# Attention loop of a two-layer hybrid encoder: one unit per step against two units per step

## The reference, cut to what matters

```python
h = layer_norm(x, ln_in_g, ln_in_b)                       # 512 tokens x 1024
for l in range(2):
    a_q, a_k, a_v, b_u, b_b, b_c, c_u, d_q, d_k, d_v = split_columns(h @ w_in[l])
    out_a = windowed_gqa_sink(a_q, a_k, a_v, sink[l])     # 4 heads, window 128, bias by distance, sink
    out_b = short_conv_mixer(b_u, b_b, b_c, conv_w[l])
    out_c = fourier_mixer(c_u)
    out_d = dense_gqa_blocks(qd, kd, d_v)                 # 4 heads, all 512 keys
    mix = concat(rms_norm(o, g_i) for o in (out_a, out_b, out_c, out_d))
    h = layer_norm(ALPHA * h + mix @ w_out[l], ...)
    h = layer_norm(ALPHA * h + square(relu(h @ w1[l])) @ w2[l], ...)
```

## Time and profile before

| | us |
|---|---|
| median of three runs | 1141.22 (1141.08 to 1141.42) |
| the profiled execution's own time | 1143.06 |
| its span, first to last instruction | 1141.4 |
| PE busy in the span | 1117.7 (98%) |
| DVE, ACT, POOL busy | 607.1 (53%), 392.0 (34%), 89.1 (8%) |
| attention loop, layer 0: first scores to first MLP matmul | 100.54 |
| attention loop, layer 1 | 101.65 |
| PE idle in the span by the page's waits (L406, L556, L362, L574, L371) | 16.3 |

### The profile page before, as it was taken

How to read it: one execution, slowest core, us unless ns; L and a number is a source line. 1 busy time by engine, 2 the same in 40 slices (tenths; PEclk the granted TensorE clock), 3 DMA queues, 4 the chain that set the end, 5 groups by cost and what they waited for, 6 DMA issues and landing times.

```text
span 1141.4 us, 15090 instructions
## 1 busy us (share of the span) xinstructions
PE 1117.7 (98%) x5486; PEld 932.9 (82%) x5486; DVE 607.1 (53%) x906; ACT 392.0 (34%) x630; POOL 89.1 (8%) x80
## 2 busy tenths in 40 slices
PE   6999999999999999999999999999999999999997
PEld 5787788898888888888888878879888888888886
DVE  6754876855235235235657467677533433434446
ACT  2433655452143133134134246543421421422320
POOL 4200222000000000000002002221000000000001
PEclk9999999999999999999999999999999999999999
DMA  7322112033114113124104420211323123222201
GB/s 288 145 105 83 38 56 75 1 118 148 74 74 148 74 74 147 74 74 148 74 3 148 148 74 20 74 38 45 148 74 146 76 74 130 85 78 110 85 28 74
DMA packets 16944, 104.90 MB, mean 92 GB/s; under 512 B 2096, under 2 KB 2528, under 8 KB 5232
## 3 DMA queue, kind: packets, MB, share of 16 engines
q1 hardware_dynamic: 15408, 97.92, 23.2%
q0 software_dynamic: 1184, 5.86, 1.6%
q10 hardware_dynamic: 288, 0.27, 0.1%
HBM read 100.90 MB, written 2.10 MB: 90 GB/s over the span
## 4 chain that ended last, share of the span: by engine, by line
PE 90%; DVE 4%; issue 2%; ACT 1%; DVEq 0%; ACTq 0%
PE bank L362 27%; PE bank L364 27%; PE bank L363 27%; PE bank L574 2%; PE bank L556 2%; PE bank L471 1%; PE bank L547 1%; PE bank L371 1%; PE bank L548 1%; ACT stage L827 1%; DVE mx L1194 1%; DVE stage L1191 1%; DVE x L949 0%; DVE x L1154 0%; DVE mx L1200 0%
## 5 line engine op out<-in xcount | busy, mean ns | idle before, releaser
L362 PE MATMUL bank<-h_hi,w_hi 128*128 128x512 f32 (+1 forms) x704 | 261.0, 371 | 1.6 <-DVE h_lo L970 1.6
L364 PE MATMUL bank<-h_hi,w_lo 128*128 128x512 f32 (+1 forms) x704 | 260.3, 370 | 0.0
L363 PE MATMUL bank<-h_lo,w_hi 128*128 128x512 f32 (+1 forms) x704 | 260.3, 370 | 0.0
L362 PE MATMUL bank<-w_hi,hid_hi 128*128 128x512 f32 x512 | 199.3, 389 | 0.0
L364 PE MATMUL bank<-w_hi,hid_lo 128*128 128x512 f32 x512 | 199.2, 389 | 0.0
L363 PE MATMUL bank<-w_lo,hid_hi 128*128 128x512 f32 x512 | 199.2, 389 | 0.0
L693 ACT CAST w_hi<-w_raw 128x2048 fp32r<-128x2048 f32 x60 | 112.3, 1908 | 243.9 <-PE bank L364 220.3
L362 PEld LDWEIGHTS bank<-h_hi,w_hi 128*128 128x128 f32 x704 | 132.6, 188 | 24.3 <-issue 1.8
L363 PEld LDWEIGHTS bank<-h_lo,w_hi 128*128 128x128 f32 x704 | 132.6, 188 | 22.5
L364 PEld LDWEIGHTS bank<-h_hi,w_lo 128*128 128x128 f32 x704 | 132.6, 188 | 22.4
L1259 DVE TENSOR_TENSOR x<-bank,x 128x512 f32<-128x512 f32 x64 | 44.2, 690 | 198.1 <-PE bank L364 197.7
(11 more groups left out here) (145 smaller groups left out, 1359.1 us busy)
## 6 DMA issues: line engine op xcount, KB each, us to landing
w_raw<-in_weights SPq DMA_DIRECT2D x86, 1024.0 KB, 4.8
rows<-in_rows POOLq DMA_DIRECT2D x4, 1024.0 KB, 5.0
w_raw<-in_weights SPq DMA_DIRECT2D x4, 512.0 KB, 6.9
out_h<-x SPq DMA_DIRECT2D x8, 256.0 KB, 2.0
x<-in_x SPq DMA_DIRECT2D x3, 512.0 KB, 7.4
dft<-in_dft SPq DMA_DIRECT2D x1, 1024.0 KB, 9.4
qk_gain<-in_qk_gain POOLq DMA_DIRECT2D x3, 192.0 KB, 3.4
dq_even<-dq_lo POOLq DMA_DIRECT2D x2, 256.0 KB, 2.9
```

What stands on the lines that cost most here:

```text
L362: pe.matmul(dst, s_hi, m_hi, start=first, stop=False)
L363: pe.matmul(dst, s_hi, m_lo, start=False, stop=False)
L364: return pe.matmul(dst, s_lo, m_hi, start=False, stop=last)
```

## The change

Steps now handle pairs of units. In step p PE makes the scores of units 2p and 2p+1, then the side items, then the values of the pair p-2, then (in even steps from 4) the turned quad, then the transposes of the pair p-1. ACT and DVE follow in kind. There are 16 pairs and 18 steps. `stage` has four places; the fourth lies over the first half of `bz`, which is free by then. The side table is written anew: two `w` items in each of the steps 0 to 11, in 13, 15 and 17, none in 12 and 14, the first turned block in step 16, the second in step 17. `mix_low` of the Fourier group is done for both halves in step 1, the query copies `dq_even` and `dq_odd` in step 3, the norm of the blocks 0 and 1 in the steps 14 to 16. On POOL the subtraction for `dq_lo` moves ahead of the first power of the quads.

```diff
-STAGES = 3
-TURN_LAG, VALUE_LAG = 1, 1
-STEPS = UNITS + VALUE_LAG
+STAGES = 4
+PAIRS = UNITS // 2
+STEPS = PAIRS + 2
...
 def quad_scaled_in(step):
-    q, rest = divmod(step - VALUE_LAG - 3, 4)
-    return q if rest == 0 and q >= 0 else None
+    return (step - 3) // 2 if step >= 3 and step % 2 else None
...
-SIDE_STEPS = {-1: [("s", 0)], 0: w_items(0, 0, 1), 4: [("s", 1)],
-              27: [("t", 0, 0), ("t", 0, 1)], 32: [("t", 1, 0), ("t", 1, 1)]}
...
+SIDE_STEPS = {-1: [("s", 0)]}
+for _g in range(3):
+    SIDE_STEPS.update({4 * _g + _t: w_items(_g, _t, _t + 1) for _t in range(TOK)})
+SIDE_STEPS[2] = SIDE_STEPS[2] + [("s", 1)]
+SIDE_STEPS.update({13: w_items(3, 0, 1), 15: w_items(3, 1, 2), 16: t_items(0), 17: w_items(3, 2, 3) + t_items(1)})
...
+                for p in range(STEPS):
+                    for u in pair(p):
+                        scores(u)
+                    for k in sides_of(p):
                         side(k)
-                    if quad_turned_in(s) is not None:
-                        turn_quad(quad_turned_in(s))
...
+                    for u in pair(p - 2):
+                        take_values(u)
+                    if quad_turned_in(p) is not None:
+                        turn_quad(quad_turned_in(p))
+                    for u in pair(p - 1):
+                        turn_probs(u)
...
+                for p in range(STEPS):
+                    if quad_turned_in(p) is not None:
+                        square_head_out(quad_turned_in(p))
+                    for u in pair(p):
+                        exponents(u)
+                    if p in (0, 1):
+                        wait(act, l, "fourier_out", p + 1)
                         wait(act, l, "square_sum", 1)
-                        square(j, co[:, j, :])
-                        mix_high(1, j, co[:, j, :])
...
+                        square(p, co[:, p, :])
+                        mix_high(1, p, co[:, p, :])
+                    for k in sides_of(p):
+                        side(k)
+                    if quad_turned_in(p) is not None:
+                        mix_high_quad(quad_turned_in(p))
+                    for u in pair(p - 1):
+                        copy_turned(u)
+                    if p == 3:
                         wait(act, l, "mix_lo", 2)
...
+                for p in range(STEPS):
+                    for u in pair(p):
+                        row_maximum(u)
+                    for k in sides_of(p):
                         side(k)
-                    if s in (2, 3):
-                        mix_low(1, s - 2, co[:, s - 2, :])
...
+                    if p == 1:
+                        mix_low(1, 0, co[:, 0, :])
+                        mix_low(1, 1, co[:, 1, :])
+                    if quad_turned_in(p) is not None:
+                        mix_low_quad(quad_turned_in(p))
+                    if quad_scaled_in(p) is not None:
+                        scale_quad(quad_scaled_in(p))
+                    if p == 14:
+                        centre(2 * l + 1, 0)
+                    if p == 15:
+                        scale(2 * l + 1, 0)
+                    if p == 16:
+                        centre(2 * l + 1, 1)
+                        scale(2 * l + 1, 1)
                 centre(2 * l + 1, 2)
```

More of the change, by code:

```diff
@@ L142 @@
 TAIL = len(SIDE)
-SIDE += w_items(3, 3, 4) + [("t", t, half) for t in (2, 3) for half in range(2)]
-NORM_AT = {24: 0, 28: 1}
+SIDE += w_items(3, 3, 4) + t_items(2) + t_items(3)
 def sides_of(step):
@@ new lines, in scores @@
+                def scores(u):
+                    in_d, j, kv, qb, k0, k1 = unit(u)
+                    if u == 0:
+                        wait(pe, l, "k_lo", 2)
+                    if u == 16:
+                        wait(pe, l, "k_lo", 4)
+                        wait(pe, l, "dq_moved", 32)
+                    if u >= 2:
+                        wait(pe, l, "probs", u - 1)
+                    q, k = slice(qb * P, (qb + 1) * P), slice(k0 * P, k1 * P)
+                    both = (dq_even, dq_odd)[kv][:, j, q] if in_d else aq[:, kv, j, q]
+                    dst = bank[u % 2][:, 0:(k1 - k0) * P]
+                    pe.matmul(dst, both, (dk_hi if in_d else ak_hi)[:, kv, k], start=True, stop=False)
+                    pe.matmul(dst, both, (dk_lo if in_d else ak_lo)[:, kv, k], start=False, stop=True).then_inc(sems["scores"], 1)
@@ L801, in split_half @@
                         done.then_inc(sems["w_hi"], 1)
[L803 to L832, removed]
-                        wait(act, l, "square_sum", 1)
-                        square(j, co[:, j, :])
-                        mix_high(1, j, co[:, j, :])
-                    if s in (5, 6):
-                        j = s - 5
-                        wait(act, l, "mix_lo", 2)
-                        wait(act, l, "dq_copied", j + 1)
-                        act.copy(dq_even[:, j, :], dq[:, j, :]).then_inc(sems["dq_hi"], 1)
-                        act.copy(dq_odd[:, j, :], dq[:, j, :]).then_inc(sems["dq_hi"], 1)
-                    for k in sides_of(s):
-                        side(k)
-                    if quad_turned_in(s) is not None:
-                        mix_high_quad(quad_turned_in(s))
-                    if s in (10, 11):
-                        split_half(12, s - 10, 24)
-                    if s in (18, 19):
-                        split_half(13, s - 18, 32)
@@ L1349, in _ @@
                         layer_norm_rstd(2 * l + 1, q - 5, q - 4)
-                    if q == 1:
+                    if q == 0:
+                        for j in range(2):
+                            wait(pool, l, "dq_hi", 2 * j + 2)
+                            pool.tensor_tensor(dq_lo[:, j, :], dq[:, j, :], dq_even[:, j, :].bitcast(F32), ALU.subtract).then_inc(sems["dq_lo"], 1)
                         wait(pool, l, "dq_lo", 2)
```

165 lines of the change are left out of this document (82 added, 83 removed).

## The result

The changed kernel took 1146.3 us (1143.44 to 1147.14, six executions) beside 1141.32 of the kernel before: ratio 1.0034, interval 1.0024 to 1.0045 (the quotient of the two medians, 1.0044, lies at its upper end). In a second measurement it was 1145.2 beside 1142.14, 1.0023 (1.0013 to 1.0032). The forecast was 1136.9. The profiled execution of after took 1143.44, its span 1141.8. Two executions with a mean granted clock of 0.44 and 0.85 (2558.97 us of the kernel before, 1248.76 of the last variant) are left out of every ratio.

A forecast was written before the change was run, and what follows sets the result against it. PE, busy 98% of the span, was taken as the bound. The two loops were to lose 10.2 us and clock drops to add 5.9, so 1141.22 - 4.3 = 1136.9 us; range 1130.5 to 1141.5.

The forecast's parts named there:

- 43 of 60 go, 3.65 us per layer: PE, both loops: 43 of 60 changes from f32 to r matmuls vanish, at 0.085 us each.
- Two Fourier remainders (0.66 each): DVE at the loop's start: two remainders of 0.66 us each, ending at 10.2, the second waiting for ACT.
- The stall before `s`: PE at the loop's start: item `s` waits 2.05 us for DVE's add of that step's first `w`.
- the lock: Rival: DVE's second remainder waits for POOL at the start, 1.1 us per layer, 1139.1 in all; chance 0.08.
- Four spans of 1.47: PE's clock drops once in each new stretch, at start and end of both loops, 4 x 1.47 = 5.9 us.
- The waits for ACT inside the loop: PE in steps 3 to 15: no wait for ACT; all 8.7 us of old stalls taken as gone.
- The end of the loop: From the scores of pair 15: new stalls of 4.5 us in sum.
- idle before the turned block 0: PE in step 16: waits 2.1 us for the first half of DVE's `scale`.
- a wait before the MLP: PE behind step 17's values: waits 1.9 us for DVE's adds with statistics and `h_lo` halves.
- the bound in the A steps: Rival: DVE takes PE's place there, A pairs keep 5.5 us instead of 5.2, 1140.5 in all; chance 0.12.
- The fourth stage: A smaller edit, said only to take waits away; priced at nothing.

The follow-up runs named there:

- the split of the groups: Kernel with all three moves, but in steps 8 to 11 PE's values stand between the two `w` items; step 11 took 6.36 us against 6.27.
- the last variant: Kernel with `s` in step 3, the end reordered and the second Fourier remainder in step 2, but `s` behind step 3's `w` items: ratio 0.9939.

## Why the prediction was wrong, step by step

**The ledger.** Forecast per loop with its clock 98.9, measured 102.5: 3.6 too much. To the start of step 4 it takes 24.65 (forecast 20.24 + 1.47), 2.9 too much; from there to the scores of pair 15, 58.48 (56.25), 2.2; from there to the MLP 19.34 (19.4 + 1.47), 1.5 too little. The parts 20.24 and 56.25 are the forecast's terms sorted by step.

**The step that failed: "43 of 60 go, 3.65 us per layer. It is the surest term."** The changes go, and each is worth its 0.09; the split of the groups shows it. But a pair gained 0.10, not 0.31 (6.38 - 6.07). I read one edge of an r group, where it starts late, and took the f32 distances of one unit (0.35, 0.80) as the price of the work in any grouping. In groups of two they are 0.80 and 1.73, 0.23 more per pair. At the price of these D pairs the missing 0.21 is some 3.4 us per layer over 16 pairs, an estimate, since the A pairs have shorter groups. The ledger leaves about 3.0 for it: the 2.2 of the middle, and 0.8 of the start's 2.9 when 0.8 of stall and 1.5 of clock are taken off and 0.2 added for the shorter waits of the scores 2 and 3. Either way it takes back most of the 3.65. That the order alone does this is shown with the other engines taken away. It is the largest part of the miss, 6 of 7.3 us in the two loops.

**"Two Fourier remainders (0.66 each)".** The stall before `s` was forecast at 2.05 and is 2.85. Without the overlap with POOL it is 1.69 of idle, about 1.85 by starts: the forecast's sum was right but for the lock, which stood among the rivals with 0.08 and a price of 1.1 per layer; holding POOL back gave 1.0. The row on which I rejected it was misread. I held POOL's 1.75 for its own length; by itself the addition takes 1.30 (the row above; before, the subtraction for `dq_lo` of the same shape takes 1.30 too). So the row, with DVE ahead by 0.13, is a POOL instruction held for 0.45 by DVE's remainder, and the trace of the kernel before already showed the lock. It also had the other order, a little earlier, with POOL's addition from 114.86 to 116.51 and DVE's remainders of another group, the first of which came behind it:

```profile
L1102 DVE SCALAR_TENSOR_TENSOR mix_lo<-bo,cols,mix_hi x2: 741/1251/1761, 115.3 to 117.0; 128x512 fp32r<-128x512 f32 x2
```

741 and 1761 ns, once more 1.0 too long. The Trainium skill, SBUF — State Buffer, section "SBUF: two separate sides", says that whichever of the two starts first keeps the shared ports for its whole instruction. The traces agree, in both orders: held DVE instructions end 0.55 after POOL's end (117.06 after 116.51, 129.33 after 128.78), and POOL's addition begun behind a DVE remainder takes 1.75 to 1.81 for 1.30.

**The clock.** Four spans of 1.47 were forecast, one at each start and end of two loops. What came is worth four such spans, but two in each layer's start, 3.0 behind the larger stall, and none at the end. That the sum of 6.0 meets the 5.9 is luck. That the drop hangs on the idle and not on the small products alone is shown: filled, it is gone; at 1.00 of idle it costs 1.6 (131.62 to 136.44 is 4.82, at the full level 3.2), at 1.69 it costs 1.6 or 3.2, at 2.70 it costs 3.0. The idle alone doesn't fix it: 0.77 ahead of the scores of pair 3 was followed by a drop in layer 1 and by none in layer 0 of the same profile. At a loop's end it appeared in one profile only (the item `s` one step later, layer 0).

**What was right.** The waits for ACT inside the loop are gone. The end of the loop is right in sum (19.34), less so in its parts: 1.4 of idle before the turned block 0 for 2.1, and the turned block 1 waits for the adds of step 17 (0.37 and 0.73), which I had priced as a wait before the MLP. DVE did not become the bound in the A steps. The fourth stage is worth nothing.

**What stays open.** The 3.6 per loop make 7.3 of the 9.4 between forecast and result. The loops' growth of 2.9 accounts for the second measurement, but the first had 5.0 between the medians. What differs between profiles outside the loops lies ahead of the first one: between the loops every profile shows 456.9 to 457.2, behind the second 361.4 to 361.6, but the first loop begins anywhere from 118.21 to 121.93, in kernels whose work up to there is the same. It begins by 119.7 where the granted clock is 1.00 from 16 to 28 us, and from 119.9 on where it is low there. An estimate from this: had the median execution of after begun its loop as the profiled one of before did, it would have taken 1143.44 + 2.63 = 1146.1, and 1146.3 was measured; the six of the kernel before, 1141.0 to 1141.65, lie 1.4 to 2.1 below its profiled one, as with an earlier start. No profile of such an execution shows it, and why an execution gets the one or the other start was not found. The low clock of before in layer 1 isn't constant either: with the fourth stage alone both loops last 100.5, so between loops without a drop in before the change costs 4.0, not 2.9.

## What to carry to other kernels

Price a reordering by measuring the whole pattern both ways, not one edge of it: an f32 group of twice the length costs more than two short ones. When work of one queue moves, ask what the engine that shares its ports is doing at that time, and in which order the two begin. The waits of 0.97 to 2.70 us on PE ahead of small products cost 1.6 to 3.2 us beyond their own length here through the clock, so first look for the waits that stand there; moving one such item turned a kernel that was 3 us slower than the old one into one that was 4 us faster. Before a record's length is taken as proof that nothing held it, compare it with the same instruction where its neighbour is idle.

## What the runs showed of the hardware

- A DVE instruction with two SBUF inputs that began behind a POOL one took 1.75 us instead of 0.74, in each of the four places read (743 became 1745 and 1767, 741 became 1759 and 1761); the other way round POOL's addition took 1.75 to 1.81 instead of 1.30 and its small product 1.48 instead of 1.01. The hold stands inside the record of the held instruction and not as idle time.
- f32 behind f32 of the same kind cost more than behind another kind of work: four transposes 0.35, eight 0.80; eight values 0.80, sixteen 1.73. Alone and in a row, eight values took 0.89 and four transposes 0.43.
- TensorE fell from 2.4 to 1.2 GHz (granted clock 0.57 over 8 us) behind idles of 2.70, 1.69, 1.00 and 0.97 us ahead of small products in the profiled executions, and not behind one of 0.80 ahead of wide r matmuls. Between 0.61 and 0.77 ahead of short work it did both (0.62 and 0.65 in the earlier trace rows, 0.77 in two layers of one profile), and two of four executions of the last variant ran as if there had been no drop.
